# Products and norms in one block, a shorter norm chain, and the first two tiles of a product taken together

## The reference

```python
def rms_norm(x, g):
    xf = x.astype(jnp.float32)
    y = xf * lax.rsqrt(jnp.mean(xf * xf, axis=-1, keepdims=True) + EPS)
    return (y * g.astype(jnp.float32)).astype(x.dtype)
def swiglu(h, w_gate, w_up, w_down):
    return (jax.nn.silu(h @ w_gate) * (h @ w_up)) @ w_down
...
    for layer in range(DEPTH):
        ...
        h = modulate(x, 0)
        x = x + HALF_STEP * (1.0 + mod[:, 0, 2]) * swiglu(h, ffn_w_gate[layer, 0], ffn_w_up[layer, 0], ffn_w_down[layer, 0])
        h = modulate(x, 1)
        ...
        x = x + (1.0 + mod[:, 1, 2]) * y.astype(x.dtype)
        h = modulate(x, 2)
        x = x + HALF_STEP * (1.0 + mod[:, 2, 2]) * swiglu(...)
    return rms_norm(x, final_norm_g)
```

## Time and profile before

| | us |
|---|---|
| median of 3 runs | 4019.63 (4016.6 to 4019.92) |
| profiled execution | 4019.48 |
| its span, first to last instruction | 4017.7 |
| PE busy | 3541.7 (88%) |
| DVE busy | 1998.4 (50%) |
| ACT busy | 1299.9 (32%) |
| mean granted clock of TensorE | 0.93 |

### The profile page before, as it was taken

How to read it: one execution, slowest core, us unless ns; L and a number is a source line. 1 busy time by engine, 2 the same in 40 slices (tenths; PEclk the granted TensorE clock), 3 DMA queues, 4 the chain that set the end, 5 groups by cost and what they waited for, 6 DMA issues and landing times. The chain is left out here.

```text
span 4017.7 us, 58426 instructions
## 1 busy us (share of the span) xinstructions
PE 3541.7 (88%) x22344; PEld 2855.6 (71%) x22344; DVE 1998.4 (50%) x2858; ACT 1299.9 (32%) x1700; POOL 302.1 (8%) x238
## 2 busy tenths in 40 slices
PE   4999999378999999988999999895498997988998
PEld 3888777357888788866677787674376886867776
DVE  7554562754554555255443433255645774255243
ACT  2432223433332333233342442232123553323231
POOL 1000000120000000010100000100001331010001
PEclk9999999589999999999999999996698998998999
DMA  6454322013554355221022223120021000212222
GB/s 244 175 187 172 104 89 81 0 32 110 187 187 171 132 188 184 103 75 63 1 89 89 84 94 104 64 87 14 0 94 40 7 8 25 101 67 79 89 94 73
DMA packets 103074, 380.31 MB, mean 95 GB/s; under 512 B 11265, under 2 KB 14977, under 8 KB 102529
## 3 DMA queue, kind: packets, MB, share of 16 engines
q1 hardware_dynamic: 102912, 378.04, 26.7%
HBM read 375.90 MB, written 2.10 MB: 94 GB/s over the span
## 5 line engine op out<-in xcount | busy, mean ns | idle before, releaser
L311 PE MATMUL bank<-h_hi,w_hi 128*128 128x512 f32 x2752 | 1095.4, 398 | 71.3 <-DVE h_lo L606 25.7
L313 PE MATMUL bank<-h_hi,w_lo 128*128 128x512 f32 x2752 | 1083.3, 394 | 0.0
L312 PE MATMUL bank<-h_lo,w_hi 128*128 128x512 f32 x2752 | 1083.1, 394 | 0.0
L211 DVE TENSOR_TENSOR w_lo<-w_raw,w_hi 128x1024 fp32r<-128x1024 f32 (+2 forms) x480 | 631.5, 1316 | 686.0 <-ACT w_hi L205 679.8
L311 PEld LDWEIGHTS bank<-h_hi,w_hi 128*128 128x128 f32 x2752 | 523.3, 190 | 221.5 <-issue 80.7
L205 ACT ACTIVATE w_hi<-w_raw 128x1024 fp32r<-128x1024 f32 (+2 forms) x480 | 528.0, 1100 | 383.6 <-PE bank L313 309.1
L313 PEld LDWEIGHTS bank<-h_hi,w_lo 128*128 128x128 f32 x2752 | 523.7, 190 | 112.6
L312 PEld LDWEIGHTS bank<-h_lo,w_hi 128*128 128x128 f32 x2752 | 525.2, 191 | 103.4
L311 PE MATMUL bank<-f_gu_hi,w_hi 128*128 128x512 f32 x704 | 277.6, 394 | 8.9 <-PEq L236 8.9
L312 PE MATMUL bank<-f_gu_lo,w_hi 128*128 128x512 f32 x704 | 276.6, 393 | 0.0
L313 PE MATMUL bank<-f_gu_hi,w_lo 128*128 128x512 f32 x704 | 276.3, 392 | 0.0
(11 more groups left out here) (569 smaller groups left out, 4400.7 us busy)
## 6 DMA issues: line engine op xcount, KB each, us to landing
w_raw<-in_gu SPq DMA_DIRECT2D x176, 512.0 KB, 4.3
ada_tiles<-in_ada SPq DMA_DIRECT2D x164, 512.0 KB, 3.8
w_raw<-in_dn SPq DMA_DIRECT2D x64, 704.0 KB, 4.1
w_raw<-in_w_ff SPq DMA_DIRECT2D x64, 512.0 KB, 3.1
w_raw<-in_w_hyb SPq DMA_DIRECT2D x36, 512.0 KB, 3.4
ada_up<-in_ada SPq DMA_DIRECT2D x7, 2048.0 KB, 26.5
w_raw<-in_w_rkv SPq DMA_DIRECT2D x24, 512.0 KB, 3.2
w_raw<-in_w_attn SPq DMA_DIRECT2D x20, 512.0 KB, 3.2
```

The source lines that it names most:

```text
L211: K.nc.vector.tensor_tensor(K.w_lo[:, half, 0:kb * P], K.w_raw[:, slot, 0:kb * P], K.w_hi[:, half, 0:kb * P].bitcast(F32), ALU.subtract).t ...
L311: nc.tensor.matmul(K.ps[bank][:], wh, hi, start=start, stop=False)
L312: nc.tensor.matmul(K.ps[bank][:], wh, lo, start=False, stop=False)
L313: last_mm = nc.tensor.matmul(K.ps[bank][:], wl, hi, start=False, stop=stop)
```

## The change

1. **One block.** Consecutive gemms, norms and set-up pieces share a `Block` (`one_block`, `open_block`, `close_block`); what the barriers had ordered is now ordered by waits on semaphores. Blocks still end ahead of the LRU and SSD pieces, ahead of attention and around RWKV. The mLSTM's heads and the product that follows them are inside one block too, and that product uses banks 4 to 7.
2. **Norm chain.** POOL adds only seven squares; PE takes the eighth square directly (four more matmuls). ACT takes the root straight from the bank with scale and bias; `root_table` loads the root's table ahead of time in most places. The diagonal is gone: PE makes the row from `rs` itself, as four matmuls with 128 columns.
3. **First two tiles together.** In a gemm with a head, the second tile is split ahead of the scaling; DVE first scales all eight chunks and then makes all `h_lo`; PE runs the hi passes of both tiles chunk by chunk as `h_hi` arrives, and then the 16 passes on `h_lo`. `rolled` writes out the first turn too.

```diff
+def one_block(K):
+
+    return nullcontext(K.block) if K.block else K.nc.Block()
...
     assert n_tiles % turn == 0 and g0 % RING == 0 and turn % RING == 0
-    with nc.Block() as block:
+    done0 = g0 + PRIMED
+    with one_block(K) as block:
...
+            def first_pair():
+                for j in range(2):
+                    pe.wait_ge(K.lo_done.sem, g0 + j + PRIMED + 1)
+                    pe_wait(pe, 0, j, j)
+                for k in range(kb):
+                    pe.wait_ge(K.h_hi_done.sem, K.h_hi_done(k + 1))
+                    for j in range(2):
+                        hi, lo, bank, start, stop = mm(k, j)
+                        wh, wl = weights(j, k)
+                        nc.tensor.matmul(K.ps[bank][:], wh, hi, start=start, stop=False)
+                        nc.tensor.matmul(K.ps[bank][:], wl, hi, start=False, stop=False)
+                for j in range(2):
+                    for k in range(kb):
+                        hi, lo, bank, start, stop = mm(k, j)
+                        pe.wait_ge(K.h_ready.sem, K.h_ready(k + 1))
+                        last_mm = nc.tensor.matmul(K.ps[bank][:], weights(j, k)[0], lo, start=False, stop=stop)
+                    last_mm.then_inc(K.tile_mm.sem, 1)
...
     def rms_pe(self, pe):
...
+            mm(total[:, t:t + 1], self.acc[:, t * P:(t + 1) * P], K.ones[:, 0:1], start=t == 0, stop=False, skip_group_check=True)
+        pe.wait_ge(K.sq_done.sem, K.sq_done(0))
+        for t in range(NT):
+            last = mm(total[:, t:t + 1], self.last[:, t * P:(t + 1) * P], K.ones[:, 0:1], start=False, stop=True, skip_group_check=True)
         last.then_inc(K.rms_sum.sem, 1)
-        pe.wait_ge(K.rms_diag.sem, K.rms_diag(1))
-        mm(K.ps[self.ROW][:], K.ones, K.diag[:].rearrange("p t k -> p (t k)"), start=True, stop=True).then_inc(K.rms_row.sem, 1)
+        pe.wait_ge(K.rms_step.sem, K.rms_step(1))
+        for t in range(NT):
+            last = mm(K.ps[self.ROW][:, t * P:(t + 1) * P], K.rs[:, t:t + 1].to_broadcast([P, P]), K.ident, start=True, stop=True)
+        last.then_inc(K.rms_row.sem, 1)
...
     def rms_act(self, act):
-        K.nc.scalar.activation(K.pad4[:], K.consts[:, 0:NT], ACT.Sqrt)
-        act.wait_ge(K.rms_step.sem, K.rms_step(1))
-        K.nc.scalar.activation(K.rs[:], K.rs[:], ACT.Sqrt).then_inc(K.rms_root.sem, 1)
+        act.wait_ge(K.rms_sum.sem, K.rms_sum(1))
+        K.nc.scalar.activation(K.rs[:], K.ps[self.SUM][:, 0:NT], ACT.Sqrt, bias=col(K, "eps"), scale=1.0 / D).then_inc(K.rms_root.sem, 1)
...
     project(K, w_down, KB_MAX, 2, mm2, nxt, lambda o: (K.coef[:, bass.ds(o, 1)]),
...
+            ready=lambda pe, j: pe.wait_ge(K.gu_lo_done.sem, low + FC - 1 + j % 2))
...
     project(K, K.dram["w_hout"], DC, 2, mm, nxt, lambda o: K.coef[:, bass.ds(o, 1)], Squares(K, "hyb", K.arena + n * S * 4),
+            ready=lambda pe, j: (pe.wait_ge(r_done, 2 * SSD_G), pe.wait_ge(lo_done[j % 2], DC)))
...
+    stream_out(K, d["w_out2"], DC, (d["w_ff10"], DC), act_out(K, mix, 0, ACT.Copy), square_mix, squares=squares,
+               ready=lambda pe, j: pe.wait_ge(lo_done, DC))
```

More of the change, by code:

```diff
@@ L171, in setup @@
     K.sq_done, K.sq_added = K.count("sq_done"), K.count("sq_added")
-    K.rms_sum, K.rms_step, K.rms_root, K.rms_diag, K.rms_row = (K.count("rms_" + n) for n in ("sum", "step", "root", "diag", "row"))
+    K.rms_sum, K.rms_step, K.rms_root, K.rms_row = (K.count("rms_" + n) for n in ("sum", "step", "root", "row"))
     K.scaled, K.h_hi_done, K.h_ready, K.x_written = (K.count(n) for n in ("h_scaled", "h_hi_done", "h_ready", "x_written"))
@@ L215, with rolled, gemm @@
 PRIMED = 4
-def rolled(eng, n, body):
-    if n > 2:
-        with eng.Fori(0, n - 1) as i:
+def rolled(eng, n, body, apart=None):
+    first = 1 if apart and n > 1 else 0
+    if first:
+        body(0, False)
+    if n - first > 2:
+        with eng.Fori(first, n - 1) as i:
             body(i, False)
-    elif n == 2:
-        body(0, False)
+    elif n - first == 2:
+        body(first, False)
     body(n - 1, True)
-def gemm(K, w, kb, n_tiles, nxt, mm, pe_wait, act_evac=None, dve_evac=None, turn=4, post=None, side=None, head=None, squares=None, fetched=RING, fetch=RING, aside=None):
+def gemm(K, w, kb, n_tiles, nxt, mm, pe_wait, act_evac=None, dve_evac=None, turn=4, post=None, side=None, head=None, squares=None, fetched=RING, fetch=RING, aside=None, slots_free=None):
     nc = K.nc
@@ L266, in body @@
                     t = turn * i + j
-                    if not (last and j == turn - 1):
+                    if head and isinstance(i, int) and t == 0:
+                        pass
+                    elif not (last and j == turn - 1):
                         split_hi(K, act, kb, (j + 1) % RING, (j + 1) % SPLIT, g0 + t + 1)
@@ L330, in _ @@
             def _(pool):
+                pool.wait_ge(K.tile_mm.sem, done0)
                 squares.clear(pool)
                 def body(i, last):
-                    for j in range(squares.per):
+                    for j in range(squares.per - last):
                         squares.add(pool, squares.per * i + j, j % 2)
@@ L454, in _ @@
             squares.clear(pool)
-            for c in range(DC):
+            for c in range(DC - 1):
                 squares.add(pool, c, c % 2)
@@ L786, in conv_evacs, with stream_out @@
     return act_evac, dve_evac
-def stream_out(K, w, n, nxt, act_evac, dve_evac=None, post=None, head=None, squares=None, fetched=RING, fetch=RING, aside=None):
+def stream_out(K, w, n, nxt, act_evac, dve_evac=None, post=None, head=None, squares=None, fetched=RING, fetch=RING, aside=None, slots_free=None, ready=None, bank0=0):
     free = K.bank_free
     def mm(k, j):
-        return K.h_hi[:, k, :], K.h_lo[:, k, :], j, k == 0, k == DC - 1
+        return K.h_hi[:, k, :], K.h_lo[:, k, :], bank0 + j, k == 0, k == DC - 1
     def pe_wait(pe, i, j, t):
         pe.wait_ge(free.sem, free(t - RING + 1))
+        if ready:
+            ready(pe, j)
     gemm(K, w, DC, n, nxt, mm, pe_wait, act_evac, dve_evac, post=post, head=head, squares=squares,
-         fetched=fetched, fetch=fetch, aside=aside)
+         fetched=fetched, fetch=fetch, aside=aside, slots_free=slots_free)
     free.base += n
@@ L1222, in hybrid_out @@
     ng = K.cols_at["ssd_norm_g"][0]
-    with nc.Block() as block:
+    lo_done = [K.sem(f"hyb_lo{n}") for n in range(2)]
+    with one_block(K) as block:
         @block.scalar
@@ L2963, in build @@
                 with stage(K):
-                    hybrid(K, nxt, head)
+                    mixed = hybrid(K, nxt, head)
+                open_block(K)
+                with stage(K):
+                    hybrid_out(K, *mixed, nxt)
             elif step == "ml":
```

192 lines of the change are left out of this document (119 added, 73 removed).

## The result

The changed kernel takes 3923.95 us (median of 4 executions, 3921.84 to 3926.27); the kernel before, run beside it, 4018.11 us. The ratio is 0.9768, 95% interval 0.9751 to 0.9785. The forecast of 3921 us was 3 us off. The profiled execution took 3924.56 us at a mean granted clock of 0.94.

The account below looks back on a forecast made before the run. PE, busy 88%, was taken to bound the kernel, leaving only its idle stretches and the slow-clock stretches behind them to win. Joints 42, late starts 19.6 and norms 36 us sum to 98, from 4019.5 to 3921 us; range 3900 to 3948.

Parts of the forecast that it names:

- Joints: Thirteen product-to-product joints: without the barrier, 28.2 us of idle time and 14.1 us of slow clock are won, together 42 us.
- The cover: At joints, the next product's first tile (5.4 or 7.5 us) hides evacuation and split, 5.6 us at worst, within 0.2 us.
- w_out2 kept its gap: One joint waits for all of `h_lo` before its first tile; 3.5 of the 31.7 us left there.
- joints aren't free: Rival: 27 joints, norms and late starts each keep about 0.5 us, eight keep slow stretches; 26 us back, 3947; chance 0.14.
- Late starts: Three products behind set-up blocks start earlier: hyb's output 6.3 us, w_z 7, w_gate2 6.3; together 19.6 us.
- Norms: Norm heads and last norm: five heads at 5.2 us each (26), the others added; together 36 us.
- The chain: Norm at f01: first matmul at +6.8 us after the last product's final matmul, before +12.2; a gain of 5.4 us.
- The pair wins nothing by itself: First two tiles at a head: the wait moves from tile two to tile three, which starts at 15.9 us, before 15.7.
- The waits for `w_lo` at the eight heads: Sign: PE waits 2 to 3 us before tile three at f01; a sum over 25 us at the heads refutes the prediction.
- The barrier at a head: Barriers at a norm, named in b2's second norm: removing them saves 0.8 us.
- Nothing for unchanged code: Stretches whose instructions stay the same: no term in the sum of 42 + 19.6 + 36 us.
- a rival for slower code: Code fetching at 27 joints: stalls above 3.6 us each make the kernel slower, 4032 at 4.1 us; chance 0.03.

Follow-up runs that it names:

- third_first: Changed kernel, but in a product with a head the third tile's split stands ahead of the first tile's evacuation on ACT and DVE; 3906.96 us.
- Early_split: no_pair plus the second tile's split ahead of root and scaling, with ACT's and DVE's first turn written out; 3911.96 us.
- barriers_back: Changed kernel with every block closed again, so each product, norm and set-up piece ends with a barrier; shorter norm chain and pair stay; 3993.82 us.
- no_pair: Changed kernel with part 3 undone: first two tiles one after the other, late second split, first turn not written out; 3926.44 us.

## Why the prediction was right

The sum was 98 us and 94.9 came. That they agree to 3 us is luck in part: the terms were off by more, on both sides. By its own terms:

- **Joints, 42 us forecast, 44.2 measured.** The cover held at every joint; the cost of a joint without a barrier was put at nothing, and was nothing. w_out2 kept its gap (4.01 us) and its slow stretch, as forecast. The rival "joints aren't free" is out.
- **Late starts, 19.6 forecast, 17.6 measured.** w_z 7.2 for 7, w_gate2 6.6 for 6.3. At hyb's output product tile two began where I had said (11.3 us after DVE's scaling starts, 859.55 - 848.25; the forecast has 872.9 - 861.5), but I had priced only the slow tile before it. Behind PE's wait of 3.84 us the clock fell anew for 6.8 us, at 0.46 x 6.8 = 3.1 us about the 2.5 us that are missing.
- **Norms, 36 forecast, 45.1 measured** (f00 to w_ff1 41.9, the last 3.1). The chain came out as worked: first matmul at +7.0 for +6.8 at f01. What was mis-sized is the pair. "The pair wins nothing by itself" is wrong as a sum over a head: tile three starts 13.6 us after the first matmul at f01, forecast 15.9. PE waited 1.08 us for its split instead of the 2 to 3 forecast, because the table load of 1.28 stood under the first tiles, and the slow stretch of the pair was 3.0 us instead of 4.8. At hyb, ml and w_ff1 the wait came out as forecast: 2.96, 3.02 and 2.47 us for 3.2, 3.2 and 2.6. The waits for `w_lo` at the eight heads sum to 14.3 us, below the 25 that would have spoken against the forecast. The mechanism, that the wait moves from tile two to tile three, was right, and third_first shows what that wait was still worth. Early_split shows that the gain isn't the order's of the passes, for which, taken alone, the sentence holds; it comes with the early split and the table loads that went, which the forecast left where they were. The barrier at a head was priced at 0.8 us: beside the new chain it costs 2.4 at f01 (barriers_back).
- **Nothing for unchanged code, 0 forecast, 12.0 us lost.** This is the step that failed. It was covered by the surplus at the heads: two errors of 9 and 12 us cancelled in the total. I had a rival for slower code, but at the joints, where nothing showed; 4.8 us went in the RWKV's long straight code, 3.5 are longer slow stretches in the mLSTM, LRU and SSD, and the rest (3.7) is open.
- The Trainium skill, "ScalarE: Activation LUTs", What ACT_TABLE_LOAD costs, has a drain of about 1380 ns at each switch. In no_pair's rows the load begins at 957.27, takes 1.28 us, and the next ACT instruction starts at 958.57; in third_first's the rounding ends at 960.37 and the load begins at 960.39. So no drain stands on either side, as the trace of before had it.

## What to carry to other kernels

Read a change of 2% in pieces cut at fixed places of the program, and include the pieces that it doesn't touch: here 12 us of a gain went missing in them, and two versions with the same time differed by 16 us at the very place of the edit. What stands ahead of a wait in an engine's order decides more than the order of the passes: moving one tile's split forward, with the turn written out and its table loads gone, was worth 14.5 us, and moving the next one's 17 (8.9 of them seen at the heads). An edit that writes out a loop's turn can do more than it says: count the instructions of each kind before and after. Before an edit is blamed, see whether it has moved a buffer or lengthened the code ahead of other stretches.

## What the hardware did that I hadn't expected

- A start of the activations' buffer 32 bytes further on than a multiple of 128 lengthened every matmul that reads it by 6.3 ns of 227, 23 us in this kernel; 64 bytes off cost a third of that, in the reads of one of the two buffers alone.
- Fulfilled waits cost PE 32 ns each (3.1 us for 96; of 24 none shows as a wait), and straight-line code of small matmuls lost 4 to 11 us to waits that no other engine ends and that changed, in part, with the place of the code.
- In code that is written out, ACT's table load ran 6.3 us ahead of the activation that needs it (955.62 and 961.88): it doesn't wait for that one's input. In the loop turns of no_pair's f01 each load of the evacuation stood behind that wait, 1.29 us ahead of its activation.
- Writing out one turn of a loop on ACT took 81 of 163 table loads out of the whole program.
